# Streaming the moving columns of every split matmul from the last to the first

## The reference

```python
def first_block(x, ...):
    h = rms_norm(x, norm_mix_pre[l])
    proj = h @ w_in[l]
    (rq, rk, rv, rg, nq, kcm, vcm, ksl, vsl, kwn, vwn, ng) = jnp.split(proj, split_at, axis=-1)
    y_ret = retention(...)          # 4 heads, decayed scores
    y_nsa = nsa(...)                # 8 heads: compressed, selected and windowed attention
    mix = jnp.concatenate([y_ret, y_nsa], axis=-1) @ w_out[l]
    x = x + rms_norm(mix, norm_mix_post[l])
    h = rms_norm(x, norm_ffn_pre[l])
    return x + rms_norm(conv_ffn(h, ffn_w_up[l], ffn_conv[l], ffn_w_down[l]), norm_ffn_post[l])

def second_block(x, ...):
    x = x + ab_mixer(rms_norm_2(x, ab_norm[0]), ...)     # mLSTM in both directions, spatial gating
    x = x + jnp.square(jax.nn.relu(rms_norm_2(x, ffn_norm[0]) @ ffn_w1[0])) @ ffn_w2[0]
    x = x + mla_mixer(rms_norm_2(x, c_norm[0]), ...)     # 16 heads of latent attention
    x = x + jnp.square(jax.nn.relu(rms_norm_2(x, ffn_norm[1]) @ ffn_w1[1])) @ ffn_w2[1]
    return rms_norm_2(x, final_norm)
```

## Time and profile before

| | us |
|---|---|
| runs, median | 1883.56 |
| runs, lowest and highest of 3 | 1883.43, 1885.21 |
| span of the profiled execution | 1881.6 |
| PE busy | 1841.5 (98% of the span), 8818 matmuls |
| DVE busy | 1155.1 (61%) |
| ACT busy | 743.9 (40%) |
| POOL busy | 226.6 (12%) |

### The profile page before, as it was taken

One profiled execution on the slowest core, in us unless ns is written; L12 is line 12 of the kernel. 1 busy time (PEld: TensorE's weight loads), 2 busy tenths in 40 slices (PEclk: granted clock), 3 DMA queues, 4 the chain that ended last, 5 costly groups with the idle time before them and its releaser, 6 DMA issues.

```text
span 1881.6 us, 24672 instructions
## 1 busy us (share of the span) xinstructions
PE 1841.5 (98%) x8818; PEld 1481.6 (79%) x8818; DVE 1155.1 (61%) x1651; ACT 743.9 (40%) x1099; POOL 226.6 (12%) x228
## 2 busy tenths in 40 slices
PE   8999999999999999999999999999999999999998
PEld 6787558888888887887888888887666788888887
DVE  7867876784765778777543434476777553444344
ACT  6365334442432454655432232334544342323232
POOL 0021453000000030000000000003477200000000
PEclk9999999999999999999999999999999999999999
DMA  6332022233333233311333333332110123333332
GB/s 215 92 133 68 1 79 90 84 94 102 92 99 101 90 113 90 90 57 56 96 101 98 93 101 94 95 100 79 46 34 25 55 90 101 95 95 100 92 98 90
DMA packets 48217, 165.68 MB, mean 88 GB/s; under 512 B 5376, under 2 KB 7424, under 8 KB 48000
## 3 DMA queue, kind: packets, MB, share of 16 engines
q1 hardware_dynamic: 46512, 161.27, 28.3%
q10 hardware_dynamic: 1616, 3.22, 0.5%
HBM read 162.38 MB, written 2.10 MB: 87 GB/s over the span
## 4 chain that ended last, share of the span: by engine, by line
PE 85%; DVE 9%; ACT 3%; issue 2%; POOL 1%; DMA 0%; DVEq 0%; ACTq 0%; SPq 0%; POOLq 0%
PE ps L695 25%; PE ps L697 25%; PE ps L696 25%; PE ps L1089 2%; DVE w_lo L2225 1%; PE ps L989 1%; DVE qk_c L2995 1%; POOL x L608 1%; ACT w_hi L1564 1%; DVE tmp L2262 1%; PE ps L917 1%; PE ps L970 1%; PE ps L1059 1%; PE ps L1355 0%; PE ps L886 0%
## 5 line engine op out<-in xcount | busy, mean ns | idle before, releaser
L1564 ACT ACTIVATE w_hi<-raw 128x1024 fp32r<-128x1024 f32 x279 | 296.1, 1061 | 760.7 <-PE ps L697 760.4
L695 PE MATMUL ps<-h_hi,w_hi 128*128 128x512 f32 (+1 forms) x1288 | 507.9, 394 | 8.1 <-DVE w_lo L2506 7.6
L697 PE MATMUL ps<-h_hi,w_lo 128*128 128x512 f32 (+1 forms) x1288 | 499.0, 387 | 0.0
L696 PE MATMUL ps<-h_lo,w_hi 128*128 128x512 f32 (+1 forms) x1288 | 498.9, 387 | 0.0
L2225 DVE TENSOR_TENSOR w_lo<-raw,w_hi 128x1024 fp32r<-128x1024 f32 x279 | 345.5, 1238 | 119.7 <-ACT w_hi L1564 118.3
L695 PEld LDWEIGHTS ps<-h_hi,w_hi 128*128 128x128 f32 x1288 | 242.5, 188 | 62.1 <-DVE w_lo L2506 7.6
L697 PEld LDWEIGHTS ps<-h_hi,w_lo 128*128 128x128 f32 x1288 | 242.3, 188 | 50.0
L696 PEld LDWEIGHTS ps<-h_lo,w_hi 128*128 128x128 f32 x1288 | 242.6, 188 | 49.2 <-issue 1.9
L695 PE MATMUL ps<-hid_hi,w_hi 128*128 128x512 f32 (+1 forms) x716 | 273.6, 382 | 1.7 <-DVE w_lo L2225 0.9
L697 PE MATMUL ps<-hid_hi,w_lo 128*128 128x512 f32 (+1 forms) x716 | 272.6, 381 | 0.0
L696 PE MATMUL ps<-hid_lo,w_hi 128*128 128x512 f32 (+1 forms) x716 | 272.6, 381 | 0.0
(11 more groups left out here) (435 smaller groups left out, 2547.6 us busy)
## 6 DMA issues: line engine op xcount, KB each, us to landing
raw<-in_panels SPq DMA_DIRECT2D x295, 512.0 KB, 3.6
x_in<-in_x SPq DMA_DIRECT2D x8, 256.0 KB, 5.5
x<-in_x ACTq DMA_DIRECT2D x1, 2048.0 KB, 9.7
out<-y SPq DMA_DIRECT2D x16, 128.0 KB, 1.8
first<-in_first SPq DMA_DIRECT2D x1, 1568.0 KB, 11.4
raw<-in_panels SPq DMA_DIRECT2D x2, 256.0 KB, 4.6
second<-in_second ACTq DMA_DIRECT2D x1, 512.0 KB, 3.5
small<-in_small ACTq DMA_DIRECT2D x1, 328.0 KB, 4.2
```

Source lines behind the costliest of these rows:

```text
L695: nc.tensor.matmul(out, a[0], b[0], start=start, stop=False)
L696: nc.tensor.matmul(out, a[0], b[1], start=False, stop=False)
L697: return nc.tensor.matmul(out, a[1], b[0], start=False, stop=stop)
L1564: nc.scalar.activation(w_high(panel, i), raw[:, panel % 4, :], ACT.Copy).then_inc(w_hi_ready, 1)
```

## The change

`product` reverses the column order of three access patterns: the result's, and both parts of the moving operand. The stationary operand, the order and the number of the matmuls, their shapes, the waits and the place of each result in PSUM stay as they are: column j of the result is still made from column j of the moving operand, but the first column that streams is the last one and the last is column 0. The order of instructions is the same on every engine.

```diff
@@ -692,9 +692,10 @@
     def _(pe):
         def product(out, a, b, start, stop):
 
-            nc.tensor.matmul(out, a[0], b[0], start=start, stop=False)
-            nc.tensor.matmul(out, a[0], b[1], start=False, stop=False)
-            return nc.tensor.matmul(out, a[1], b[0], start=False, stop=stop)
+            out, high, rest = out[:, ::-1], b[0][:, ::-1], b[1][:, ::-1]
+            nc.tensor.matmul(out, a[0], high, start=start, stop=False)
+            nc.tensor.matmul(out, a[0], rest, start=False, stop=False)
+            return nc.tensor.matmul(out, a[1], high, start=False, stop=stop)
 
         def w(panel, a, b, i=None):
             return w_high(panel, i)[:, a:b], w_low(panel, i)[:, a:b]
```

## The result

| | before | after |
|---|---|---|
| runs, median, us | 1883.66 | 1921.17 |
| lowest, highest | 1883.43, 1885.21 | 1921.01, 1921.35 |
| span of the profiled execution | 1881.6 | 1919.4 |

The ratio is 1.0197, with a 95% interval of 1.0183 to 1.0212: the change costs 37.5 us, 2%. The time lies in the range given, but not in the likeliest case.

The account below looks back on a forecast made before the run. TensorE, busy almost throughout at its upper clock, was taken to bound the kernel. Both edits were priced at zero: 1881.6 + 0 profiled, 1883.6 us for the runs, whose median lies 2.0 us above; range 1877 to 2080 us, chance 0.80.

Parts of the forecast that it names:

- the likeliest case: Whole kernel: reversal costs nothing, 1883.6 us; no change (1880 to 1887) had chance 0.64.
- What bounds it: TensorE, busy 1841.5 of 1881.6 us: whatever a matmul of `product` gains or loses, the kernel gains or loses.
- ScalarE's wait for the last matmul of a product: Wait of ScalarE's rounding for `product`, 760.4 us in 234 pieces before; claimed to stay near 760 us.
- the sum for both edits: Reversed read and reversed write in `product` together: zero added, 1881.6 + 0 profiled, 1883.6 for the runs.
- The two edits: In each `product` matmul, the moving operand read downwards and the result written and added to downwards; zero for both.
- The bounds: Per `product` matmul: from below 13.5 ns vanishing, 98 us less; from above one column in two cycles, 0.87 ns per column.
- the second rival: Fixed price per `product` matmul, for start or turn back: 13.5 ns once (1981 us) or twice (2080); chance 0.12.
- The signs of the prediction: Feed-forward step at 512 columns: 0.227 us free, 0.240 fixed price, 0.440 half rate; at 288: 0.133, 0.147, 0.253.
- fixed part: In each `product` matmul, what is left of the 0.227 us step after 512 columns at 0.4167 ns: 13.5 ns.
- Half rate and worse: All 7242 `product` matmuls: half rate 3330 to 3368 us, it or between 0.14; worse, some 6340 us, 0.06.
- The 36 us that this rival counted as slack: Steps over the starts of all 7242 `product` matmuls above columns plus fixed part, mostly attention; at most absorbable at half rate.

Follow-up runs that it names:

- e3: Bare-stream follow-up in the whole kernel: against the changed kernel, each group of four neighbouring columns reversed within itself, groups rising, in all three patterns; 1883.79 us (0.9997).
- e2: Changed kernel with the result's columns alone reversed, the moving operand rising; 1883.91 us (ratio 1.0003).
- the serpentine stream: Kernel of its own with back-to-back fp32r matmuls, reversed and plain in turn, against all plain or all reversed; steps of 227 and 233 ns in turn.
- e8: Changed kernel, all three patterns reversed, with h and all activations behind it 32 bytes further on, w_hi and w_lo unmoved; 1920.86 us (1.0195).
- the bare stream: Kernels of their own, 24 matmuls back to back per form, computing nothing of the reference; 512 columns plain 226.67 ns, reversed 233.24; 256 columns 120.00 and 118.29.

## Why the prediction was right and wrong

**What bounds it: right.** A price of 6.2 ns on a matmul came through to the kernel almost whole (39.9 us on the steps, 37.5 in the time); steps with a wait gave back 1.4 us. One sign was misplaced: ScalarE's wait for the last matmul of a product was to stay near 760 us in any case, and went to 802.1, since each of these waits lasts until a panel's last matmul, and the matmuls got longer.

**The likeliest case, no change: wrong.** The step that failed is the one that took the sum for both edits as zero: "what the change takes away from it is only the sign of the step", and a mechanism that fetches by aligned group "has as little to do downwards as upwards". Inside a group of four words that held: the order is free (e3, 1883.79 us). Between the groups it did not: their order counts, with rising words inside them too (233.24 ns for groups of four in falling order, against 226.67). What the runs showed in place of zero is 6.2 ns on each 512-column matmul, 39.9 us. The argument also looked at the moving stream by itself. The earlier trace rows has the load of the next stationary block beside every matmul, and I priced it only by its length (0.19 us, inside the step), not as something whose place could matter. For a rising stream its place does matter, as the shifts of the stationary block alone show. Whether it has any part in the falling stream's loss, no run shows.

**The two edits: one right, one wrong.** The write downwards is free, as said (e2), also from an odd first word. The read isn't.

**The bounds.** The measured price per matmul, 6.2 ns, lies between the 0 and the half rate of the bounds, at about half of the 13.5 ns by which the second rival was priced. Its time, 1887 to 2080, is where the result fell, but its mechanism isn't the cause, so that the range held the result is luck. It wasn't a longer start nor a turn back: the serpentine stream paid nothing for turning, and 256 and 320 columns pay nothing at all. Its term was named per matmul, and the runs show one that changes with the width (1.9 ns at 288, 0 at 320, 6.6 at 512). The signs of the prediction would have told: the step in the feed-forward stretch became 0.234 us, between the marks for free (0.227) and for one more fixed part (0.240), and with 288 columns it stayed at 0.133, not 0.147. Taking the "fixed part" as fixed was itself too simple: in groups of 16 it is gone, and in bf16 the step is 215.8 ns, 2.5 above the columns, in place of 13.3.

**Half rate and worse: wrong here, but not empty.** Reading every second column does give 453 ns, twice the plain step. A falling stream of neighbours doesn't. The 36 us that this rival counted as slack over the starts of all 7242 are those of the steps from one product to the next; with the 137 steps from a product to another matmul it is some 47 us (and the earlier trace rows show eight matmuls of `product`, not seven). Neither changes its rank.

**The rules that were cited.** The rule of the Trainium skill, "SBUF — State Buffer", section "SBUF: two separate sides", that accesses to one 16-byte line go at full rate, fits the free reversal in groups of 4 words, and fails on the whole reversal: four hits per line, yet 233.3 ns. The sentence of the Trainium skill in "Advanced Engine Details and Errata", section "PSUM Cachelines", doesn't catch a falling result: 1883.91 us. A rule that I should have weighed stands in the Trainium skill, "TensorE: Matmul & The Clock Gate", section "Step-by-step: what each phase is for": loading the next tile's weights "doesn't steal SBUF read bandwidth from the running matmul". For fp32r at full width the measurement doesn't fit it: the step is 226.67 ns, and 233.33 with nothing but the stationary block moved 4 words on.

**What stays open.** Why a falling stream can't reach 226.67 ns at any of 18 places isn't settled. Two readings stand. It may lose the same good meeting of the two reads as a shifted rising stream: the losses are nearly equal and don't add (e8). Or falling from group to group has a limit of its own: the step stays at 233.3 ns or a little above wherever the stationary block lies and however few columns it has. No run took the stationary load away from an fp32r stream, which would decide between them. The number of stationary columns speaks against a simple count of collisions in any case. The loss in groups of 16 is the moving read's own and has no explanation here.

No fp32r form in any run stepped faster than 226.67 ns at 512 columns. Reversing the 256-column products alone would be worth under 1 us by the bare stream (456 x 1.7 ns) and wasn't run.

## What to carry to other kernels

Where TensorE is full, give the moving and the stationary fp32r tiles starts that agree modulo 256 bytes: here that alone is worth 2%, and a harmless 32 bytes of padding in one place can take it away. (That holds for starts moved by whole 32 bytes; with both moved by 4, 8 or 16 bytes the bare stream took 238.9, 233.7 and 230.1 ns.) In 512-column products, let the moving columns rise from one group of four words to the next; the order of the result's columns is free. When a change alters how one operand is read, price it with a bare stream of the same form, which gave the kernel's step to the nanosecond, and vary in it the place of everything else that is read in the same time.

## What was not expected of the hardware

- An fp32r stream settles: with both operands 8 words on, some ten steps of 224 to 236 ns come before it stays at 227. The unshifted form does so too when it follows a bf16 stream (steps of 224 to 236 ns, at 227 from the eleventh on) or a shifted one.
- A strided read costs by bytes in bf16, but otherwise than in fp32r: every second, fourth and eighth column take 225.9, 451.7 and 900.0 ns in bf16 (215.8 plain; the granted clock fell from 1.00 to 0.50 some three steps into the last form, and the step was 900 ns before and after), every second and fourth 453.2 and 461.3 in fp32r. Sixteen bytes from column to column are thus read twice as fast in fp32r as in bf16.
- Groups of 16 and 32 columns reversed inside cost nothing in bf16 (215.9 ns).
